# One decay matrix, L by a transpose, and the norms of q and the last convolution moved behind the inverse's start

## What is computed

```python
q, k: l2-normalised outputs of a causal convolution of width 4 and silu; v: the same without the norm
g = jnp.cumsum(g, axis=-1)                        # log decays, within a chunk
decay = jnp.where(incl, jnp.exp(jnp.where(incl, gdiff, 0.0)), 0.0)     # gdiff[i,j] = g[i] - g[j]
L = jnp.where(strict, jnp.einsum("bhnid,bhnjd->bhnij", k_beta, k) * decay, 0.0)
rhs = jnp.concatenate([v_beta, k_beta * jnp.exp(g)[..., None]], axis=-1)
sol = lax.linalg.triangular_solve(L, rhs, left_side=True, lower=True, unit_diagonal=True)
qk = jnp.einsum("bhnid,bhnjd->bhnij", q, k) * decay
```

## Time and profile before

| | |
|---|---|
| median of 3 runs | 1740.15 us (1738.11 to 1740.58) |
| profiled execution: its time | 1740.75 us |
| profiled execution: first to last instruction (span) | 1738.9 us |
| PE busy / DVE / ACT / POOL | 97% / 72% / 40% / 52% of the span |
| chain that ended last | 90% PE, 6% DVE, 2% ACT |

### The profile page before, as it was taken

The page is one execution under the profiler, slowest core; times in us unless marked ns, Lnnn a source line. Parts: engine busy times, 40 slices in busy tenths (PEclk is TensorE's granted clock), DMA queues, the critical chain, the costliest instruction groups (busy, mean ns, idle before and its releaser), DMA issues.

```text
span 1738.9 us, 25635 instructions
## 1 busy us (share of the span) xinstructions
PE 1680.7 (97%) x7938; PEld 1393.7 (80%) x7938; DVE 1245.3 (72%) x3050; ACT 701.5 (40%) x1044; POOL 905.1 (52%) x710
## 2 busy tenths in 40 slices
PE   6999979987999999999999999999999999999997
PEld 5777769976888888888888888888888888888886
DVE  7658877584139999899899522223888888888886
ACT  5454565534233444444444444333333333333333
POOL 0232302043330177778777877761676776767730
PEclk9999989998999999999999999999999999999999
DMA  9422393353225644444444444466999999999993
GB/s 353 176 82 74 117 418 132 122 216 111 85 91 174 214 146 145 146 146 145 145 146 145 145 145 145 135 228 225 337 345 372 358 376 367 359 377 350 380 342 140
DMA packets 149363, 376.21 MB, mean 216 GB/s; under 512 B 32048, under 2 KB 64944, under 8 KB 146096
## 3 DMA queue, kind: packets, MB, share of 16 engines
q1 hardware_dynamic: 114480, 308.04, 50.0%
q0 software_dynamic: 34816, 67.41, 10.8%
HBM read 312.25 MB, written 63.11 MB: 216 GB/s over the span
## 4 chain that ended last, share of the span: by engine, by line
PE 90%; DVE 6%; ACT 2%; issue 1%; DVEq 1%; DMA 0%; SPq 0%; ACTq 0%
PE bank L1095 16%; PE bank L1096 16%; PE bank L1097 16%; PE bank L1494 10%; PE bank L1498 10%; PE bank L1496 10%; PE bank L1111 1%; PE bank L1113 1%; PE bank L1112 1%; PE bank L1295 1%; PE bank L1310 1%; PE bank L1454 1%; DVE modr L1568 1%; DMA xn<-in_x 0%; PE bank L1320 0%
## 5 line engine op out<-in xcount | busy, mean ns | idle before, releaser
L661 POOL DMA_INDIRECT gate_scratch<-merged,idx_cell x384 | 433.0, 1128 | 212.3 <-issue 125.3
L1095 PE MATMUL bank<-act_hi,whi 128*128 128x512 f32 x1312 | 514.5, 392 | 0.4 <-DVE act_lo L1590 0.4
L1096 PE MATMUL bank<-act_lo,whi 128*128 128x512 f32 x1312 | 511.1, 390 | 0.0
L1097 PE MATMUL bank<-act_hi,wlo 128*128 128x512 f32 x1312 | 511.1, 390 | 0.0
L1983 DVE TENSOR_TENSOR wlo<-raw,whi 128x1024 fp32r<-128x1024 f32 x254 | 309.9, 1220 | 180.2 <-ACT whi L1009 178.6
L1494 PE MATMUL bank<-whi,chi 128*128 128x512 f32 x768 | 298.8, 389 | 0.0
L1496 PE MATMUL bank<-wlo,chi 128*128 128x512 f32 x768 | 298.8, 389 | 0.0
L1498 PE MATMUL bank<-whi,clo 128*128 128x512 f32 x768 | 298.8, 389 | 0.0
L1095 PEld LDWEIGHTS bank<-act_hi,whi 128*128 128x128 f32 x1312 | 246.9, 188 | 51.6 <-DVE act_lo L1590 1.1
L1097 PEld LDWEIGHTS bank<-act_hi,wlo 128*128 128x128 f32 x1312 | 246.6, 188 | 51.5
L1096 PEld LDWEIGHTS bank<-act_lo,whi 128*128 128x128 f32 x1312 | 246.8, 188 | 50.1
(11 more groups left out here) (323 smaller groups left out, 1833.4 us busy)
## 6 DMA issues: line engine op xcount, KB each, us to landing
raw<-in_expert_tiles SPq DMA_DIRECT2D x256, 512.0 KB, 4.0
act_scratch<-aout SPq DMA_DIRECT2D x128, 256.0 KB, 2.1
gate_scratch<-zeros SPq DMA_DIRECT2D x24, 1024.0 KB, 22.4
a_in<-act_scratch SPq DMA_DIRECT2D x128, 192.0 KB
g_in<-gate_scratch SPq DMA_DIRECT2D x128, 192.0 KB, 7.0
raw<-in_in_tiles SPq DMA_DIRECT2D x28, 512.0 KB, 3.4
modr<-in_mod_tiles SPq DMA_DIRECT2D x16, 512.0 KB, 12.1
modz<-in_mod_tiles SPq DMA_DIRECT2D x16, 512.0 KB, 6.9
```

Source lines behind the costliest of these rows:

```text
L661: g.indirect_dma_start(out=gate_cells, out_offset=bass.IndirectOffsetOnAxis(ap=idx_cell[:, b, k:k + 1], axis=0), in_=merged[:, b, k:k + 1] ...
L1095: mm(out_bank[:], whi[:, slot, w], act_hi[:, k, :], start=(k == 0), stop=False)
L1096: mm(out_bank[:], whi[:, slot, w], act_lo[:, k, :], start=False, stop=False)
L1097: last = mm(out_bank[:], wlo[:, slot, w], act_hi[:, k, :], start=False, stop=(k == KD - 1))
```

## The change

- `gB` and its copy are gone: PE takes the log decays as weights directly, as a broadcast of one column (`decay_rows`).
- DVE makes only `QKT`, ACT only its exp. `a_products(t)` multiplies it with the gram (one instruction of 128x512), PE transposes the result (`a_transposes`), and `first_level` multiplies the transpose by beta (one instruction). The transposes of L and of `Tm` swap their banks.
- The norm sums of k are made one step earlier, ahead of tile 27. The rows of decays and the sums of q are interleaved differently, and the sum n = 7 is last.
- Tile 27's bank is copied by ACT to `state`, and `conv(11)` reads it from there, after `first_masked`. The memset of `state` follows it.
- ACT's inverse norms of q follow the decays' exps, and DVE's four `qk_normed` of q stand in the inverse's steps 0 to 3. The products of q and k go from steps 4 to 7 to steps 5 to 8; `VK_STEPS` stays.
- `hi(29)` moves on ACT from the last slot to behind the copies of `TT`.

```diff
-        QK_STEPS = (4, 5, 6, 7)
+        QK_STEPS = (5, 6, 7, 8)
         VK_STEPS = (9, 11, 13, 15)
...
@@ ACT
-            for n in range(8):
-                act.wait_ge(s_l2, n + 1)
-                sc.activation(l2r[:, L2_ORDER[n], :], bank[SUM_BANK[n]][:], ACT.Ln,
-                              bias=eps_t).then_inc(s_l2r, 1)
+            for n in range(4):
+                norm_log(n)
+            act.wait_ge(s_used, T_OUT)
+            sc.copy(state[:], bank[1][:]).then_inc(s_v3, 1)
+            for n in range(4, 8):
+                norm_log(n)
...
             for n in range(4):
                 inverse_norm(n)
             for t in range(NB):
-                act.wait_ge(s_du[0], t + 1)
-                sc.activation(LM[:, t, :], LM[:, t, :], ACT.Exp, scale=-1.0).then_inc(s_de, 1)
-            for n in range(4, 8):
-                inverse_norm(n)
-            act.wait_ge(s_du[1], NB + 1)
+                act.wait_ge(s_du, t + 1)
+                sc.activation(QKT[:, t, :], QKT[:, t, :], ACT.Exp).then_inc(s_de, 1)
+            act.wait_ge(s_du, NB + 1)
             for t in range(NB):
                 last = sc.activation(egT[:, t, :], bank[ROW_BANK[t]][:], ACT.Exp)
             last.then_inc(s_de, 1)
-            for t in range(NB):
-                sc.activation(QKT[:, t, :], QKT[:, t, :], ACT.Exp)
...
+            for n in range(4, 8):
+                inverse_norm(n)
...
+            hi(T_OUT + 1)
+            act.wait_ge(s_conv, 11)
             act.wait_ge(s_conv, 12)

             def silu_v(h):
+                if h == H - 1:
+                    act.wait_ge(s_conv, 12)
...
@@ PE
-                if s == H * NB + 1:
+                if s == H * NB:
                     for n2 in range(4):
                         norm_sums(n2)
...
+            def decay_rows(t):
+                for h in range(H):
+                    last = mm(bank[ROW_BANK[t]][:, hs(h)],
+                              g16(G_LOG)[:, 4 * t + h:4 * t + h + 1].to_broadcast([P, P]),
+                              masks[:, M_U, :], start=True, stop=True)
+                last.then_inc(s_row, 1)
...
+            pe.wait_ge(s_oa, H * NB)
+            pe.wait_ge(s_glog, 1)
+            mm(bank[7][:, 0:16], masks[:, M_U, :], g16(G_LOG), start=True, stop=True).then_inc(s_gc, 1)
+            pe.wait_ge(s_conv, 11)
+            decay_rows(0)
             norm_sums(4)
...
+            def a_transposes(t):
+                if t == 0:
+                    pe.wait_ge(s_de, NB + 1)
+                pe.wait_ge(s_A, t + 1)
+                for h in range(H):
+                    last = nc.tensor.transpose(bank[t][:, hs(h)], LM[:, t, hs(h)], ident[:])
+                last.then_inc(s_AT, 1)
...
@@ DVE
-                for out, m, ready in ((LM, M_NOT_STRICT, s_du[0]), (QKT, M_NOT_U, s_du[1])):
-                    for h in range(H):
-                        last = stt(out=out[:, t, h * HD:(h + 1) * HD], in0=row[:, h, :],
-                                   scalar=g16(G_CUM)[:, 4 * t + h:4 * t + h + 1], in1=masks[:, m, :],
-                                   op0=ALU.subtract, op1=ALU.add)
-                    last.then_inc(ready, 1)
+                for h in range(H):
+                    last = stt(out=QKT[:, t, h * HD:(h + 1) * HD], in0=row[:, h, :],
+                               scalar=g16(G_CUM)[:, 4 * t + h:4 * t + h + 1], in1=masks[:, M_NOT_U, :],
+                               op0=ALU.subtract, op1=ALU.add)
+                last.then_inc(s_du, 1)
...
-            def first_level(t):
+            def a_products(t):
                 dve.wait_ge(s_kg, t + 1)
                 dve.wait_ge(s_de, t + 1)
-                for h in range(H):
-                    w = slice(h * HD, (h + 1) * HD)
-                    last = stt(out=LM[:, t, w], in0=LM[:, t, w],
-                               scalar=g16(G_BETA)[:, 4 * t + h:4 * t + h + 1], in1=bank[4 + t][:, w],
-                               op0=ALU.mult, op1=ALU.mult)
-                last.then_inc(s_L, 1)
+                tt(LM[:, t, :], QKT[:, t, :], bank[4 + t][:], ALU.mult).then_inc(s_A, 1)
+
+            def first_level(t):
+                dve.wait_ge(s_AT, t + 1)
+                tt(by_head(LM[:, t, :]), by_head(bank[t][:]), bc(g16(G_BETA), t), ALU.mult).then_inc(s_L, 1)
...
-            for n in range(6):
+            for n in range(4):
                 qk_normed(n)
+            for t in range(NB):
+                a_products(t)
             for t in range(NB):
                 first_level(t)
                 if t >= 1:
                     first_masked(t - 1)
-                if t >= 2:
-                    qk_normed(t + 4)
             first_masked(NB - 1)
+            dve.wait_ge(s_v3, 1)
+            conv(11)
+            v.drain()
+            v.memset(state[:], 0.0).then_inc(s_st, 1)
...
             for n in range(5 * NB):
                 updated(n)
+                if n < 4:
+                    qk_normed(4 + n)
```

More of the change, by code:

```diff
@@ L1227, in hs @@
                 return slice(h * HD, (h + 1) * HD)
-            norm_sums(4)
-            pe.wait_ge(s_oa, H * NB)
-            pe.wait_ge(s_gB, 1)
-            mm(bank[7][:, 0:16], masks[:, M_U, :], g16(G_LOG), start=True, stop=True).then_inc(s_gc, 1)
-            for t in range(NB):
-                if t == 0:
-                    pe.wait_ge(s_conv, 11)
-                elif t < 3:
-                    pe.wait_ge(s_l2r, t)
-                else:
-                    pe.wait_ge(s_conv, 12)
-                for h in range(H):
-                    last = mm(bank[ROW_BANK[t]][:, hs(h)], gB[:, 4 * t + h, :], masks[:, M_U, :],
-                              start=True, stop=True)
-                last.then_inc(s_row, 1)
-                for n in {0: (5, 6), 1: (7,)}.get(t, ()):
-                    norm_sums(n)
+            def decay_rows(t):
[9 more added lines that the diff above has]
+            decay_rows(0)
+            norm_sums(4)
+            pe.wait_ge(s_l2r, 1)
+            decay_rows(1)
+            pe.wait_ge(s_l2r, 2)
+            decay_rows(2)
+            norm_sums(5)
+            norm_sums(6)
+            pe.wait_ge(s_v3, 1)
+            decay_rows(3)
+            norm_sums(7)
             pe.wait_ge(s_l2n, 4)
@@ L1342, in join_t @@
                 last.then_inc(s_tt, 1)
+            for t in range(NB):
+                a_transposes(t)
+            for t in range(NB):
+                first_transposes(t)
             for n in range(6 * NB + 1):
@@ L1733, in _ @@
             v.tensor_copy(g16(G_CUM), bank[7][:, 0:16]).then_inc(s_gcc, 1)
-            v.memset(state[:], 0.0).then_inc(s_st, 1)
             v.drain()
```

50 lines of the change are left out of this document (28 added, 22 removed).

## The result

| | before | after |
|---|---|---|
| median of 6 runs each, on one chip | 1740.35 us (1737.68 to 1741.20) | 1745.85 us (1743.55 to 1746.39) |
| ratio after / before | | 1.0030 (95% interval 1.0019 to 1.0040) |
| profiled execution: time, span | 1740.75, 1738.9 us | 1746.3, 1744.5 us |
| busy PE / DVE / ACT / POOL | 97 / 72 / 40 / 52% | 97 / 71 / 40 / 52% |

The change makes the kernel 5.5 us slower; 5.4 was forecast. DVE's busy time over the whole kernel is 3.4 us smaller (1245.3 and 1241.9 us), and none of it shortened the kernel.

A forecast was written before the change was run, and what follows sets the result against it. PE, 90% of the chain, was taken to bound the kernel. Mark 2.2, clock 1.0 and two stalls of 1.1 each summed to +5.4 us, moving the median from 1740.15 to 1745.5 us, range 1741.5 to 1748.2.

The forecast's parts named there:

- Up to the norms of k: Norm sums to k's norms: last logarithm 2.4 us later, DVE's arguments 4.1 us shorter, grams start only 0.7 us earlier.
- Grams and A: PE's grams: half clock after a 5.2 us rest, 6.03 us as before; first_level(0) 4.0 us later behind all grams.
- rival A: PE's clock does not fall in its rest before the grams: mark -0.3, total +1.9 us (1742.0); chance 0.12.
- First levels: DVE's first levels save 1.8 us and one norm of q 0.6, so the last Tm is 1.6 us later than before.
- conv(11): Last convolution on DVE, 3.1 us, no longer hidden; ACT's kept wait for it delays the first level_t to 259.0 us.
- M1: Start of PE's first level_t, counted from the start of the attention's last transposes; forecast 2.2 us later.
- D: ACT's wait for the convolution has no effect because DVE is quicker: +1.6 us at the first level_t; no chance given.
- the mark: Start of PE's first level_t, 256.81 us before, ending the forecast's first part; forecast +2.2 us.
- The clock at the inverse's start: Half clock on PE lasting beyond the first level_t costs 0 to 3.4 us, taken as +1.0.
- Rival C: PE's clock stays at half long after the first level_t: 2.2 + 3.4 + 2.2 = +7.8 us (1747.9); chance 0.13.
- The two stalls: PE waits at the first vk_transposes for decayed_qk, +1.1 us, and at the second for DVE behind POOL's split, +1.1.
- Rival B: DVE's 16-column instruction goes ahead of POOL's split: last term -0.95 instead of +1.1, total +3.4 us (1743.5); chance 0.18.

The follow-up runs named there:

- e6: Changed kernel with the exps of k's inverse norms straight behind their logarithms and k normed in the last attention slot; 1739.33 us, 0.9998 of the kernel before.
- e1: Changed kernel without ACT's unconditional wait for all 12 convolutions ahead of its first PM copy; 1.0046 of the kernel before.
- e4: Changed kernel with the last convolution back in its old slot, reading its bank, nothing copied to state; 1.0031 of the kernel before.
- e5: Changed kernel with the transposes of A woven into the grams instead of behind all of them; 1.0028 of the kernel before.
- e9: Kernel before with one line of the change alone, the scores one step later (steps 5 to 8); 0.9987 of the kernel before.
- e2: Changed kernel with the four v and k transposes one step later (steps 10, 12, 14, 16); 1.0058 of the kernel before.
- e3: Changed kernel with POOL's two splits behind the decays of q waiting for the first scaled_vk; 1.0049 of the kernel before.
- e7: Changed kernel with k's norms early, ACT's early convolution wait removed and v and k transposes one step later; 1736.65 us, 0.9980 of the kernel before.
- e8: Kernel before, with both decay matrices, given the early norms of k, q's norms between the first levels; 1.0001 of the kernel before.
- e12: e7 with DVE's first-level masks behind all four first levels instead of between them; 0.9940 of the kernel before.

## Why the prediction was right

Both ends came out, +5.4 and +5.5 us, and each step can be checked. The steps are right in kind; that the totals meet within 0.1 us is luck, as the sum below shows. Moments of after are moved by -0.98 us (212.57 - 211.59) to the axis of before.

*Up to the norms of k.* The attention's last product ended at 224.25 (forecast 224.3), the last logarithm began at 232.33 (232.2), the norms of k at 234.99 (234.85), and the grams at 237.54 (237.4). This chain of small terms held within 0.15 us. DVE's 4.1 us of saved arguments were off the path, as said: e6 shows what they waited for.

*Grams and A.* The rest of 5.25 us ahead of the grams did make the clock fall; rival A (0.12) is out. But the grams took 6.38 us, not 6.03. Half clock ended at about 244.2, which is 243.2 on the axis of before, where it had ended at 243.1; the grams started 0.6 earlier, so 5.7 us of them lay in it instead of 5.0, and half of the 0.7 was lost. `first_level(0)` began at 244.73 (forecast 244.2), +4.5 us instead of +4.0: this is where the forecast first missed.

*First levels.* From there to the last `Tm` it took 9.20 us (254.91 - 245.71), as the forecast's savings of 1.8 and 0.6 had it (11.55 - 2.4 = 9.15). The last `Tm` came +2.15 us later, not +1.6: the term mis-sized is the grams (0.14 for their start, 0.35 for their clock), not the first levels.

*conv(11).* 2.98 us (forecast 3.1), as its first instruction took 0.48 from SBUF instead of 0.74 from the bank. M1 +2.63 (forecast +2.2). e1 and e4 show the part of the wait: 0.4 to 0.45 of it, where 0.6 was forecast, so D (no effect of the wait) is out. The rest of the mark, the +2.15 at the last `Tm`, comes for its larger part from the order of grams and transposes (e5). `hi(29)` ran from 257.29 to 258.34 on ACT, covered as said.

*The clock at the inverse's start.* Half clock lasted until 261.3; the first `level_t` took 1.40 us to the next row instead of 0.89: +0.5, where I took +1.0 between 0 and 3.4. Rival C (+3.4) is out.

*The two stalls.* First `vk_transposes` 1.03 (forecast 1.1). The second: the 16-column instruction came 0.75 us behind the split's start (forecast 0.6) and was held 1.47 us (1.95), as POOL's two splits took 4.67 us here and not 5.13: +0.52 instead of +1.1. Rival B, where it slips in ahead, did not come up. e9 and e2 show that both come from the step of the scores alone, and e3 that POOL's split is what holds DVE.

*The sum.* 2.63 + 0.51 + 1.03 + 0.52 = 4.69 of the 4.89 at M2. The missing 0.2 is in how a wait is counted, from the end of the row before: from start to start the two stalls are 1.19 and 0.56, and the sum is 4.89. Against the forecast's 2.2 + 1.0 + 1.1 + 1.1 that is +0.4 at the mark, -0.5 for the clock, and -0.5 for the second stall, which partly cancel. The rest of the 5.5 of the medians (0.6) I can't place: in the profiles 0.98 us lie ahead of M0, whose place varies over 2.9 us between kernels, and -0.3 behind M3. The mechanism accounts for 4.9 us, and the forecast met 5.5.

## What to carry to other kernels

Before halving an engine's work, ask what that engine waits for next: here DVE got rid of 4 us and then waited for the norms of k, whose exps stood on ACT behind logarithms nobody needed yet. With this order mended (e6) the change to one matrix costs no time, and with its two waits mended too (e7) the kernel is 3.4 us under the one before; with nothing mended it only adds a transpose to the chain. Whether one matrix is the better base is open, since e8 carried losses of its own. An operation that is put "inside" a busy stage must be free of waits on both sides: a wait that is kept from the old place (ACT's for convolution 12), or a table of steps moved by one (the scores), turned hidden work into 0.4 and 1.5 us of PE's time. And a split on POOL (2.3 to 2.6 us) held DVE in both places tried, at the short instruction on `gsm` and at `masked`, which reads two SBUF tiles, so moving it can only pay if it lands beside something else: `scaled_vk`, which reads a bank, took its 0.68 us an instruction beside the second split of the kernel after (289.43 to 291.30).

## What the runs showed of the hardware

**The granted clock makes groups of times.** Stretches at 1.2 GHz in this stage lasted 3.4 us (before, 212.4 to 215.8), 6.8 us (236.3 to 243.1 and 249.9 to 256.8), 10.2 us (e3, 248.9 to 259.2) and 17 us (e8). In e6, e7 and e12, where PE rested 0.8 us ahead of the grams, the clock was full from the grams until 244.9 or later. And the time differs in steps between executions of one kernel, with the mean clock: five of e6's eleven runs lie at 1740.5 to 1740.6 us with a mean clock of 0.988, four at 1736.2 to 1737.6 with 0.990 to 0.993, two between. A gain of 2 us is about what one stretch of 3.4 us costs where PE sets the pace (1.7 us), and one profile of each kernel can't show it in the total.

**A table load is 1.28 us with nothing behind it:** in the kernel after the exps start 0.02 us after it (235.31). Going to exp and back to the logarithm cost e6 two more of them, both in idle time.

**DVE's `masked` is held beside POOL's decay of q too.** It took 1.71 us instead of 0.69 at 284.32 in the kernel after, beside POOL's operations on q, and 1.72 in the kernel before (277.98), 1.73 in e2, 1.72 in e3. In the kernel after, DVE is idle for 1.24 us behind it (before `updated` at 287.26), so it costs nothing there.
